# Decoder step on one core: 32 modulation steps spread over units 1 to 37 of the prompt attention, and the choice of the sample's blocks moved from units 10-16 to 18-27

## The chip, the cores and the metric

The kernel runs on one core of a Trainium2 chip. The metric is the device time of one execution in microseconds (us), as the median of several runs. TensorE is called PE here, VectorE DVE, ScalarE ACT, GpSimd POOL and SyncE SP.

## The reference

One layer of a decoder is computed for a prompt of 256 tokens and for a sample group of 8 sequences with one new token each. Both share the weights. Everything is float32. What matters for this change:

```
def _layer(x, c, pos, mixer, w_ada, b_ada, norm1_g, w_in, w_br_nsa, w_br_dil, w_out, ...):
    mod = jnp.einsum('bd,de->be', jax.nn.silu(c), w_ada) + b_ada          # w_ada: 2048 x (6*2048)
    shift1, scale1, gate1, shift2, scale2, gate2 = jnp.split(mod[:, None, :], 6, axis=-1)
    h = _rmsnorm(x, norm1_g) * (1 + scale1) + shift1
    q_nsa, kv_nsa, g_nsa, q_dil, kv_dil, g_merge = _project(h, w_in, pos)
    o_nsa, o_dil, states = mixer(q_nsa, kv_nsa, g_nsa, q_dil, kv_dil)
    ...
    x = x + gate1 * mix
    h = _rmsnorm(x, norm2_g) * (1 + scale2) + shift2
    ...
    x = x + gate2 * jnp.einsum('btf,fd->btd', f, w_down)

def _mixer_sample(...):
    o_cmp, p_cmp = _cmp_attend(q_nsa, kvc, pos)
    idx = _select_blocks(p_cmp, pos, ns)          # the 16 best of 33 blocks of 64 tokens, per sequence and kv head
    ...
    o_sel = _sel_attend(q_nsa, kvg, idx, pos)     # attention over the chosen blocks only
```

`shift1` and `scale1` are needed before the projection. The other four parts of `mod` (gate1, shift2, scale2, gate2) are needed only after the attention. `w_ada` holds 2048 x 2048 float32 for each part, 16 MB.

## The kernel before

Each engine has a program of its own in `program(...)`, written out by hand; what stands later in an engine's program runs later, and engines meet by semaphores (`mark` raises one, `wait_ge(*x.at(...))` waits for it). Before the stretch of this change lies the projection (PE lines 842 to 844), which ends at about 549 us; behind it lie the sample's attention (PE lines 960 to 1107), the merge and output products, SwiGLU and the down projection.

**The prompt attention** is a list `UNITS` of `NU` = 40 units. A unit is one head and one tile of 128 queries: units 0 to 7 are the dilated heads ("d", 4 heads by 2 tiles), units 8 to 39 the 16 NSA heads ("n", by 2 tiles). Even units see 128 keys in each branch, odd ones 256. PE's loop (line 905) is a software pipeline: in iteration u it issues

- `scores(u)`: lines 875 and 876 (n) or 880 (d). It needs DVE's maximum of unit u-1, since the bank is the same;
- one **modulation step** `ada(NA1 + u)`, line 732, for u below 32;
- `probs(u-1)`: transposes of the normalized probabilities, line 888. It needs DVE's `p` of unit u-1;
- `pv(u-2)`: products with the values, line 900.

Between `scores(u)` and `probs(u)` lies a chain of DVE (mask and maximum, L1923, L1925, L1928), ACT (exponentials, L1451) and DVE again (L1931 to L1942). DVE goes through the units in order, so it starts unit u+1 only after unit u's `p`.

**Modulation steps.** There are 6 parts of 8 steps (`ADA_STEPS` = 8). A step multiplies two k tiles of silu(c) with 2 x 128 rows of `w_ada`, one load of 2 MB. The first two parts (steps 0 to 15, `NA1` = 16) are done long before. The 32 steps of this text are the last four parts; they are counted here from 0 to 31. Their weights go through three slots: SP loads step k's weights as soon as PE has done step k-3 (`ada_load`, line 530). After the eighth step of a part, ACT copies the sum out (`ada_out`, L1260), PE turns it (`ada_turn`, L743) and DVE adds the bias (`ada_mod`, L1693). The first step of the next part waits for ACT's copy.

**The choice of the sample's blocks** (`select` on DVE, lines 1838 to 1906, and some PE and ACT instructions between units) first clears and fills the sample's queries in unit 9 (`sample_q`). Then it multiplies them with the compressed keys (PE L928, L931, in bank 7), softmaxes, sums, ranks 33 blocks against each other (DVE L1894 to L1902, on 16 x 1089 elements) and makes the mask `am`. The constants for it (`c_sample`, `before_c`, lines 560 and 561) are loaded on SP's queue behind the fourteenth modulation load.

**What hangs on it.** POOL gathers the cached pages of the sample's sequences (`selected_gathers`, line 654, 2 MB each): page 0 after `sample_q`, pages 1, 2, 3 after the modulation steps 30, 31 and 29, since they land in those slots, pages 4 and up after PE has used page w-4. SP's first window load waits for `am`, the next two for the scores of unit 39 (line 564). The sample's attention on PE starts with `turn_keys(0)` (L960) after unit 39 is done.

Of the kernel before, what the change touches and what calls it, by code (L numbers as in the profile page):

```python
# [186 lines left out]
def program(nc, i_, o_, ctx, seen):  # L187
# [188 lines left out]
    ADA_PARTS, ADA_K = 6, 2  # L376
    ADA_STEPS = KT // ADA_K
# [124 lines left out]
    NU = len(UNITS)  # L502

# [184 lines left out]
    def _(pe):  # L688
# [216 lines left out]
        for u in range(NU + 2):  # L905
            if u < NU:
                scores(u)
            if u == 0:
                pe.wait_ge(*act_.at("tm", LASTN))
            if NA1 + u < NA:  # L910
                ada(NA1 + u)
            if 1 <= u <= NU:
                probs(u - 1)
            if u >= 2:
                pv(u - 2)
            if u >= ADA_STEPS + 1 and u % ADA_STEPS == 1 and u <= NA - NA1 + 1:
                if u == 17:
                    pe.wait_ge(*dve_.at("am"))
                    pe.wait_ge(*act_.at("cpt"))
                ada_turn(ADA_FIRST + u // ADA_STEPS - 1)  # L920
            if u == 11:
                pe.wait_ge(sample_const, 16)
                pe.wait_ge(kv_loaded, 32)
                pe.wait_ge(*dve_.at("sample_q"))
                pe.wait_ge(*dve_.at("mod", ADA_FIRST))
                for b2 in range(2):
                    for c in range(4):
                        mm(bank[7][32 * c:32 * c + 32, 0:NBS], qb[:, 2 * c + b2, :], kcS[:, 2 * c + b2, 0:NBS],  # L928
                           start=(b2 == 0), stop=(b2 == 1))
                pe.wait_ge(*dve_.at("gx"))  # L930
                mm(bank[7][:, P:P + 192], const("rowsel2")[0:B, :], gx[0:B, :], start=True, stop=True).then_inc(*pe_.mark("cs"))  # L931
            if u == 13:
                pe.wait_ge(*dve_.at("cp"))
                mm(bank[7][0:H, 0:NBS], const("group"), pcmp[:, 0:NBS], start=True, stop=True).then_inc(*pe_.mark("imp"))
            if u == 14:
                pe.wait_ge(*dve_.at("cpg"))
                turn(bank[7][0:NBS, P:2 * P], pcmp[:, 0:NBS], ident).then_inc(*pe_.mark("cpt"))
            if u == 16:
                pe.wait_ge(*dve_.at("sel"))
                pe.wait_ge(*act_.at("cpt"))  # L940
                mm(bank[7][:, 2 * P:3 * P], const("spread")[0:H, :], selx[0:H].rearrange("p c j -> p (c j)"), start=True, stop=True)\
                    .then_inc(*pe_.mark("spread"))
# [293 lines left out]
    def _(act):  # L1236
# [203 lines left out]
        for u in range(NU + 2):  # L1440
            if u >= ADA_STEPS and u % ADA_STEPS == 0 and u <= NA - NA1:
                ada_out(ADA_FIRST + u // ADA_STEPS - 1)
# [18 lines left out]
            if u == 12:  # L1461
                act.wait_ge(*dve_.at("cm"))
                A(pcmp[:, 0:NBS], bank[7][:, 0:NBS], ACT.Exp, bias=stat_n[:, 1:2], scale=SC_N,
                  accum_out=dstat[:, 0:1]).then_inc(*act_.mark("ce"))
            if u == 14:
                act.wait_ge(*pe_.at("cpt"))
                cp(ptc[0:NBS, :], bank[7][0:NBS, P:2 * P]).then_inc(*act_.mark("cpt"))
# [185 lines left out]
    def _(dve):  # L1653
# [189 lines left out]
        def select(u):  # L1843
# [21 lines left out]
            if u == 10:  # L1865
# [3 lines left out]
            if u == 11:  # L1869
# [7 lines left out]
            if u == 12:  # L1877
# [4 lines left out]
            if u == 13:  # L1882
# [9 lines left out]
            if u == 14:  # L1892
# [4 lines left out]
            if u == 15:  # L1897
# [6 lines left out]
            if u == 16:  # L1904
# [3 lines left out]
        for u in range(NU):  # L1908
# [48 lines left out]
            if u >= ADA_STEPS + 2 and u % ADA_STEPS == 2 and u <= NA - NA1 + 2:  # L1957
                ada_mod(ADA_FIRST + u // ADA_STEPS - 1)
            select(u)


# [279 lines left out]
```

## Time and profile before

| | us |
|---|---|
| median of 3 runs | 2106.77 (2106.63 to 2110.05) |
| the profiled execution | 2110.02 |
| its span | 2107.7 |
| PE busy in the span | 1952.0 (93%) |
| DVE, ACT, POOL busy | 977.2, 772.9, 58.4 |
| DMA moved | 512.53 MB, mean 243 GB/s |

The span is the time from the first to the last instruction of the profile. Times below count from its start. A PE row of the timeline that says "[1.45 <-DVE ...]" tells that PE sat idle for 1.45 us before it and what ended that. "PEclk" is the clock that PE was granted: 1.00 is 2.4 GHz and 0.50 is 1.2 GHz. Matmuls of float32 are recorded twice, so a step of 8 matmuls shows as x16.

### The profile page before, as it was taken

How to read it: one execution, taken by the hardware profiler on the slowest of the kernel's cores; microseconds unless marked ns; L12 is line 12 of the kernel's file. 1: busy time of each engine (PE TensorE's matmuls, PEld its weight loads, DVE VectorE, ACT ScalarE, POOL GpSimd, SP SyncE). 2: the span in 40 equal slices, each digit the busy share in tenths (PEclk: the TensorE clock that was granted, in tenths of full speed). 3: DMA queues.
4: the chain of work that ended last, by engine and by line, in shares of the span. 5: the costliest groups of instructions: out<-in, count | busy, mean ns of one | idle time of the engine just before them, and what ended most of it. 6: DMA issues, size and time to landing. Idle time of an engine off the chain costs nothing.

```text
span 2107.7 us, 36811 instructions
## 1 busy us (share of the span) xinstructions
PE 1952.0 (93%) x15765; PEld 1786.1 (85%) x15765; DVE 977.2 (46%) x1730; ACT 772.9 (37%) x1232; POOL 58.4 (3%) x108
## 2 busy tenths in 40 slices
PE   6988999999879997999999996999999999999967
PEld 3667999999645565699999996999999999999966
DVE  3355445554346532264444756344444433645425
ACT  2345333334324432253333434333333333533322
POOL 0000000000000000000000000000000000000010
PEclk9998989999989959889999997999999999999989
DMA  9981769889899916665555653686767676578791
GB/s 372 422 288 61 214 208 313 280 275 301 338 393 372 412 43 251 229 191 186 180 182 170 219 172 141 235 271 230 267 231 267 233 244 207 196 243 270 249 315 56
DMA packets 336137, 512.53 MB, mean 243 GB/s; under 512 B 8753, under 2 KB 310105, under 8 KB 319497
## 3 DMA queue, kind: packets, MB, share of 16 engines
q1 hardware_dynamic: 316146, 368.53, 52.5%
q0 software_dynamic: 5248, 125.73, 15.1%
q10 hardware_dynamic: 14640, 16.80, 2.4%
q8 instruction: 76, 1.25, 0.2%
q14 instruction: 27, 0.22, 0.0%
HBM read 504.29 MB, written 98.91 MB: 286 GB/s over the span
## 4 chain that ended last, share of the span: by engine, by line
PE 84%; DMA 9%; DVE 4%; ACT 2%; issue 1%; SPq 0%; DVEq 0%; ACTq 0%
PE bank L1129 17%; PE bank L1130 17%; PE bank L1131 17%; PE bank L842 5%; PE bank L843 5%; PE bank L844 5%; DMA piece<-in_w_ada 4%; PE bank L732 3%; PE bank L769 2%; DMA piece<-in_w_down 2%; PE bank L900 2%; PE bank L875 1%; DMA mem<-in_cache_sel_kv,runs 1%; DMA mem<-in_const 1%; PE bank L888 1%; PE bank L960 1%
## 5 line engine op out<-in xcount | busy, mean ns | idle before, releaser
L1129 PE MATMUL bank<-piece,piece 128*128 128x264 f32 x3072 | 877.8, 286 | 50.6 <-DVE piece L2050 26.0
L1130 PE MATMUL bank<-piece,piece 128*128 128x264 f32 x3072 | 877.0, 285 | 0.0
L1131 PE MATMUL bank<-piece,piece 128*128 128x264 f32 x3072 | 876.6, 285 | 0.0
L2055 DVE TENSOR_TENSOR piece<-piece,piece 128x2048 fp32r<-128x2048 f32 (+2 forms) x216 | 440.9, 2054 | 504.5 <-ACT piece L1541 504.5
L1129 PEld LDWEIGHTS bank<-piece,piece 128*128 128x128 f32 x3072 | 582.4, 190 | 52.2 <-DVE piece L2055 24.6
L1541 ACT CAST piece<-piece 128x2048 fp32r<-128x2048 f32 (+2 forms) x216 | 368.7, 1715 | 589.0 <-PE bank L1131 509.6
L1131 PEld LDWEIGHTS bank<-piece,piece 128*128 128x128 f32 x3072 | 582.4, 190 | 0.0
L1130 PEld LDWEIGHTS bank<-piece,piece 128*128 128x128 f32 x3072 | 582.0, 189 | 0.0
L842 PE MATMUL bank<-piece,piece 128*128 128x264 f32 (+1 forms) x816 | 241.1, 295 | 0.0
L843 PE MATMUL bank<-piece,piece 128*128 128x264 f32 (+1 forms) x816 | 234.9, 288 | 0.0
L844 PE MATMUL bank<-piece,piece 128*128 128x264 f32 (+1 forms) x816 | 234.5, 287 | 0.0
L1271 ACT CAST piece<-piece 128x2048 fp32r<-128x2048 f32 (+1 forms) x51 | 96.3, 1887 | 213.2 <-PE bank L844 213.2
L842 PEld LDWEIGHTS bank<-piece,piece 128*128 128x128 f32 (+1 forms) x816 | 155.2, 190 | 1.7
L843 PEld LDWEIGHTS bank<-piece,piece 128*128 128x128 f32 (+1 forms) x816 | 155.2, 190 | 0.8
L844 PEld LDWEIGHTS bank<-piece,piece 128*128 128x128 f32 (+1 forms) x816 | 154.9, 190 | 0.2
L1713 DVE TENSOR_TENSOR piece<-piece,piece 128x2048 fp32r<-128x2048 f32 (+1 forms) x51 | 115.6, 2267 | 82.3 <-ACT piece L1271 82.2
L732 PE MATMUL bank<-piece,mem 128*32 128x512 f32 x768 | 101.8, 651 | 19.3 <-DMA piece<-in_w_ada 14.0
L1737 DVE COPY mem<-bank 64x256 f32<-64x256 f32 x128 | 54.0, 422 | 66.0 <-PE bank L758 52.4
L769 PE MATMUL bank<-mem 128*128 128x128 f32 x512 | 63.5, 285 | 7.0 <-DVE mem L1737 3.1
L732 PEld LDWEIGHTS bank<-piece,mem 128*32 128x32 f32 x768 | 21.1, 114 | 57.4 <-issue 33.5
L769 PEld LDWEIGHTS bank<-mem 128*128 128x128 f32 x512 | 61.6, 200 | 8.5 <-ACT mem L1282 5.9
L1282 ACT COPY mem<-bank 64x256 f32<-64x256 f32 x128 | 47.0, 367 | 53.0 <-PE bank L758 50.4
(324 smaller groups left out, 1449.7 us busy)
## 6 DMA issues: line engine op xcount, KB each, us to landing
piece<-in_w_ada SPq DMA_DIRECT2D x48, 2048.0 KB, 12.3
out_s_dil<-in_cache_dil_kv POOLq DMA_DIRECT2D x64, 1023.5 KB, 6.3
piece<-in_w_in SPq DMA_DIRECT2D x50, 1024.0 KB, 8.2
piece<-in_w_gate SPq DMA_DIRECT2D x22, 2048.0 KB, 8.1
piece<-in_w_up SPq DMA_DIRECT2D x22, 2048.0 KB, 8.1
piece<-in_w_down SPq DMA_DIRECT2D x32, 1408.0 KB, 6.7
piece<-in_w_in SPq DMA_DIRECT2D x16, 2048.0 KB, 8.2
piece<-in_w_out SPq DMA_DIRECT2D x8, 2048.0 KB, 8.7
```

The costliest lines, as they stand in the source:

```text
L732: last = mm(ada_banks(part_)[0][32 * j:32 * j + 32, :], siluP[:, step * ADA_K + k, :], slot(ada_slot(a), ADA_K, D)[:, k, j * 512:(j + 1) * ...
L769: last = mm(bank[0][:, sh * P:(sh + 1) * P], w1p[:, kv, l, :, :].rearrange("p j e -> p (j e)"), KS0[:, sh * 1024 + l * P:sh * 1024 + (l + ...
L842: mm(out, w_high[:, k, :], half_tile(n1_high[k]), start=(k == 0), stop=False)
L843: mm(out, w_high[:, k, :], half_tile(n1_low[k]), start=False, stop=False)
L844: last = mm(out, w_low[:, k, :], half_tile(n1_high[k]), start=False, stop=(k == KT - 1))
L1129: mm(out, w_high[:, k, :], half_tile(x_high[k]), start=(start and k == first_tile), stop=False)
L1130: mm(out, w_high[:, k, :], half_tile(x_low[k]), start=False, stop=False)
L1131: last = mm(out, w_low[:, k, :], half_tile(x_high[k]), start=False, stop=(stop and k == len(x_high) - 1))
L1271: cp(chunk_piece(chunk_high(n), n, F32R), chunk_piece(chunk_low(n), n, F32)).then_inc(*act_.mark("w_high", n))
L1541: cp(half_chunk(buffer, k_tiles), raw).then_inc(done, 1)
L1713: v.tensor_tensor(chunk_piece(a, n, F32R), chunk_piece(a, n, F32), chunk_piece(chunk_high(n), n, F32R).bitcast(F32), ALU.subtract).then_in ...
L2055: v.tensor_tensor(half_chunk(a, k_tiles, f, CW), raw, half_chunk(buffer, k_tiles).bitcast(F32), ALU.subtract)\
```

## The change

`STEP_AT` maps a unit to the step that it carries. With `NF` = 32 and `NU` - 2 = 38, step i goes to unit 1 + 38i//32: units 1 to 6, 8 to 12, 14 to 18, 20 to 25, 27 to 31 and 33 to 37. Units 0, 7, 13, 19, 26, 32, 38 and 39 carry none. `PART_END` names the units with the last step of a part: 9, 18, 28 and 37 (before: 7, 15, 23, 31). ACT's copy comes one iteration later, PE's turn two and DVE's bias three, as before; the last bias comes after DVE's loop. The choice of the sample's blocks keeps its order, but stands in units 18 (`gx`) and 22 to 27 in place of 10 to 16. `sample_q` stays in unit 9. Loads, their order on SP's queue, gathers and all sizes are the same.

```diff
+    NF = NA - NA1
+    STEP_AT = {1 + i * (NU - 2) // NF: NA1 + i for i in range(NF)}
+    PART_END = {1 + (ADA_STEPS * (i + 1) - 1) * (NU - 2) // NF: ADA_FIRST + i for i in range(NF // ADA_STEPS)}
...
# PE
-            if NA1 + u < NA:
-                ada(NA1 + u)
+            if u in STEP_AT:
+                ada(STEP_AT[u])
...
-            if u >= ADA_STEPS + 1 and u % ADA_STEPS == 1 and u <= NA - NA1 + 1:
-                if u == 17:
+            if u - 2 in PART_END:
+                if PART_END[u - 2] == ADA_FIRST + 2:
                     pe.wait_ge(*dve_.at("am"))
                     pe.wait_ge(*act_.at("cpt"))
-                ada_turn(ADA_FIRST + u // ADA_STEPS - 1)
-            if u == 11:
+                ada_turn(PART_END[u - 2])
+            if u == 22:
                 pe.wait_ge(sample_const, 16)
                 pe.wait_ge(kv_loaded, 32)
                 pe.wait_ge(*dve_.at("sample_q"))
-                pe.wait_ge(*dve_.at("mod", ADA_FIRST))
+                pe.wait_ge(*dve_.at("mod", ADA_FIRST + 1))
...
-            if u == 13:
+            if u == 24:
...
-            if u == 14:
+            if u == 25:
...
-            if u == 16:
+            if u == 27:
...
# ACT
-            if u >= ADA_STEPS and u % ADA_STEPS == 0 and u <= NA - NA1:
-                ada_out(ADA_FIRST + u // ADA_STEPS - 1)
+            if u - 1 in PART_END:
+                ada_out(PART_END[u - 1])
...
-            if u == 12:
+            if u == 23:
...
-            if u == 14:
+            if u == 25:
...
# DVE, select(u): 10 -> 18, 11 -> 22, 12 -> 23, 13 -> 24, 14 -> 25, 15 -> 26, 16 -> 27
...
-            if u >= ADA_STEPS + 2 and u % ADA_STEPS == 2 and u <= NA - NA1 + 2:
-                ada_mod(ADA_FIRST + u // ADA_STEPS - 1)
+            if u - 3 in PART_END:
+                ada_mod(PART_END[u - 3])
             select(u)
+        ada_mod(ADA_PARTS - 1)
```

How the instructions stand on PE, at three places. In the rows 32x512 x8 is one modulation step; 128x15 ends the scores of a unit, 64x128 are the products with the values. Lines of the changed kernel are three higher than those of the kernel before (735 for 732, 878 for 875, 891 for 888, 903 for 900).

First place, PE in units 11 and 12 before, where the sample's products with the compressed keys (928, 931) stand behind step 11:

```order
L732 MATMUL bank<-piece_61,mem 32x512 x8
L888 MATMUL bank<-mem 128x128 x2
L888 MATMUL bank<-mem 15x128
L900 MATMUL bank<-mem 64x128 x5
L928 MATMUL bank<-mem 32x127 x8
L931 MATMUL bank<-mem 128x192
L875 MATMUL bank<-mem 128x128 x2
L876 MATMUL bank<-mem 128x15
L732 MATMUL bank<-piece_57,mem 32x512 x8
```

The same products in the changed kernel, in unit 22 behind step 18:

```order
L735 MATMUL bank<-piece_57,mem 32x512 x8
L891 MATMUL bank<-mem 128x128 x4
L891 MATMUL bank<-mem 15x128
L903 MATMUL bank<-mem 64x128 x3
L931 MATMUL bank<-mem 32x127 x8
L934 MATMUL bank<-mem 128x192
L878 MATMUL bank<-mem 128x256 x2
```

They moved back by eleven units and seven steps.

Second place, PE around unit 26 of the changed kernel, between the steps of units 25 and 27:

```order
L735 MATMUL bank<-piece_57,mem 32x512 x8
L891 MATMUL bank<-mem 128x128 x2
L891 MATMUL bank<-mem 15x128
L903 MATMUL bank<-mem 64x128 x5
L940 MATMUL bank<-mem 127x128
L878 MATMUL bank<-mem 128x128 x2
L879 MATMUL bank<-mem 128x15
L891 MATMUL bank<-mem 128x128 x4
L891 MATMUL bank<-mem 15x128
L903 MATMUL bank<-mem 64x128 x3
L878 MATMUL bank<-mem 128x256 x2
L735 MATMUL bank<-piece_59,mem 32x512 x8
```

Two rounds of transposes and value products stand between two steps; in the kernel before there is one round between any two steps.

Third place, PE behind the last step, before:

```order
L732 MATMUL bank<-piece_59,mem 32x512 x8
L888 MATMUL bank<-mem 128x128 x2
L888 MATMUL bank<-mem 15x128
L900 MATMUL bank<-mem 64x128 x5
L875 MATMUL bank<-mem 128x128 x2
L876 MATMUL bank<-mem 128x15
L888 MATMUL bank<-mem 128x128 x4
L888 MATMUL bank<-mem 15x128
L900 MATMUL bank<-mem 64x128 x3
```

and in the changed kernel, down to the scores of unit 39:

```order
L735 MATMUL bank<-piece_59,mem 32x512 x8
L891 MATMUL bank<-mem 128x128 x2
L891 MATMUL bank<-mem 15x128
L903 MATMUL bank<-mem 64x128 x5
L878 MATMUL bank<-mem 128x128 x2
L879 MATMUL bank<-mem 128x15
L891 MATMUL bank<-mem 128x128 x4
L891 MATMUL bank<-mem 15x128
L903 MATMUL bank<-mem 64x128 x3
L878 MATMUL bank<-mem 128x256 x2
```

Before, the scores of units 32 to 39 stand behind the last step; after, those of units 38 and 39 alone.

## Rows read from the trace of the kernel before

**Rows 1.** The page's slices: granted clock and DMA share, 40 slices of 52.7 us.
```profile
PEclk9998989999989959889999997999999999999989
DMA  9981769889899916665555653686767676578791
```

**Rows 2.** Windows: stretch, length, busy PE, PEld, DVE, ACT, POOL, clock, DMA share, GB/s.
```profile
578.80:725.80 147.00, 128.38 (x928) 71.11 (x928) 75.60 (x444) 55.37 (x226) 1.97 (x2) 0.93 0.97 392
727.70:754.80 27.10, 26.18 (x117) 19.31 (x113) 13.10 (x88) 11.65 (x49) 1.88 (x2) 0.62 0.47 188
754.80:775.90 21.10, 18.84 (x71) 13.24 (x70) 7.37 (x48) 7.54 (x31) 0.00 (x0) 0.50 0.15 50
740.00:760.00 20.00, 20.00 (x75) 14.82 (x74) 9.85 (x67) 8.44 (x36) 0.00 (x0) 0.50 0.03 10
660.00:720.00 60.00, 59.32 (x447) 32.91 (x443) 30.58 (x209) 27.99 (x118) 0.00 (x0) 1.00 1.01 410
```

**Rows 3.** PE's timeline, steps 4 to 6 in the dilated units: start, length, operation, idle before.
```profile
573.82 1.92 PE L732 MATMUL bank<-piece,mem 128*32 128x512 f32 x16 [0.41 <-DMA piece<-in_w_ada]
578.78 1.92 PE L732 MATMUL bank<-piece,mem 128*32 128x512 f32 x16 [0.27 <-DMA piece<-in_w_ada]
583.75 1.92 PE L732 MATMUL bank<-piece,mem 128*32 128x512 f32 x16 [0.56 <-DMA piece<-in_w_ada]
```

**Rows 4.** PE's timeline, unit 11 and the step behind it.
```profile
623.99 1.08 PE L928 MATMUL bank<-mem 128*32 128x127 f32 x16 [11.67 <-DMA mem<-in_const]
...
627.31 3.64 PE L732 MATMUL bank<-piece,mem 128*32 128x512 f32 x16
```

**Rows 5.** PE's timeline, three steps in a row at the full clock (units 19 to 21).
```profile
668.32 1.93 PE L732 MATMUL bank<-piece,mem 128*32 128x512 f32 x16
670.17 0.55 PE L888 MATMUL bank<-mem 128*128 128x128 f32 x3
...
677.47 1.92 PE L732 MATMUL bank<-piece,mem 128*32 128x512 f32 x16
```

**Rows 6.** PE's timeline, units 15 and 16, where DVE ranks the blocks.
```profile
649.20 0.71 PE L875 MATMUL bank<-mem 64*128 64x128 f32 x4 [1.45 <-DVE mem L1925]
...
651.86 3.15 PE L732 MATMUL bank<-piece,mem 128*32 128x512 f32 x16 [1.83 <-ACT mem L1260]
```

**Rows 7.** PE's timeline from the last step to the sample's first transposes.
```profile
725.80 1.92 PE L732 MATMUL bank<-piece,mem 128*32 128x512 f32 x16 [1.12 <-DMA piece<-in_w_ada]
...
734.11 0.73 PE L888 MATMUL bank<-mem 128*128 128x128 f32 x3 [0.92 <-DVE mem L1942]
734.77 2.58 PE L900 MATMUL bank<-mem 128*64 128x128 f32 x10
...
744.87 0.90 PE L888 MATMUL bank<-mem 128*128 128x128 f32 x3
...
754.76 0.90 PE L888 MATMUL bank<-mem 128*128 128x128 f32 x3
```

**Rows 8.** DVE's timeline: two of the rankings, then unit 32's first and last operations.
```profile
644.34 1.27 DVE L1894 TENSOR_TENSOR mem<-mem 16x1089 f32<-16x1089 f32 x1
...
652.37 1.27 DVE L1898 TENSOR_TENSOR mem<-mem 16x1089 f32<-16x1089 f32 x1
...
730.49 0.29 DVE L1923 CUSTOM_DVE_ANT_0 mem<-bank,mem 128x128 f32<-128x128 f32 x1 [1.27 <-PE bank L876]
...
733.43 0.62 DVE L1942 TENSOR_SCALAR mem<-mem 128x128 f32<-128x128 f32 x3
```

**Rows 9.** POOL's timeline: the gathers of pages 1, 2 and 4.
```profile
722.16 0.97 POOL L654 DMA_INDIRECT mem<-in_cache_sel_kv,runs  x1 [115.83 <-PE bank L732]
728.02 0.94 POOL L654 DMA_INDIRECT mem<-in_cache_sel_kv,runs  x1 [4.89 <-PE bank L732]
...
795.46 0.94 POOL L654 DMA_INDIRECT mem<-in_cache_sel_kv,runs  x1 [65.26 <-PE bank L1010]
```

**Rows 10.** PE's timeline, the sample's first scores, where the clock rises again.
```profile
780.65 1.77 PE L971 MATMUL bank<-mem 128*32 128x512 f32 x8
```

**Rows 11.** DMA issues by line, window 578.8 to 725.8: count, KB each, us to landing.
```profile
piece<-in_w_ada SPq DMA_DIRECT2D x24, 2048.0 KB, 11.5
```

More of the change, by code:

```diff
@@ L1864, in select @@
                 v.tensor_copy(qz[:, :, 0:64:9], dqnew).then_inc(*dve_.mark("sample_q"))
-            if u == 10:
+            if u == 18:
                 dve.wait_ge(sample_const, 16)
@@ L1868, in select @@
                                 const("pairof")[0:B].unsqueeze(2).broadcast_to([B, 4, 48]), ALU.mult).then_inc(*dve_.mark("gx"))
-            if u == 11:
+            if u == 22:
                 dve.wait_ge(*pe_.at("cs"))
@@ L1876, in select @@
                     .then_inc(*dve_.mark())
-            if u == 12:
+            if u == 23:
                 dve.wait_ge(*act_.at("ce"))
@@ L1881, in select @@
                 v.tensor_scalar(pcmp[:, 0:NBS], pcmp[:, 0:NBS], dstat[:, 0:1], None, ALU.mult).then_inc(*dve_.mark("cp"))
-            if u == 13:
+            if u == 24:
                 dve.wait_ge(*pe_.at("imp"))
@@ L1891, in select @@
                 link(v.tensor_tensor(sc, sc, const("force")[0:H], ALU.add))
-            if u == 14:
+            if u == 25:
                 dve.wait_ge(order_loaded, 16)
@@ L1896, in select @@
                 link(v.tensor_reduce(rank, rk[0:H], AX.X, ALU.add))
-            if u == 15:
+            if u == 26:
                 link(v.tensor_tensor(rk[0:H], other, mine, ALU.is_gt))
@@ L1903, in select @@
                                 const("selmask")[0:H].unsqueeze(2).broadcast_to([H, 4, 32]), ALU.mult).then_inc(*dve_.mark("sel"))
-            if u == 16:
+            if u == 27:
                 dve.wait_ge(*pe_.at("spread"))
```

## The prediction, made before the changed kernel had run

> **What bounds the kernel now.** I began with the page's slices [rows 1]: PE's granted clock is 9 or 8 tenths nearly everywhere, but 5 in the slice from 738 to 790 us, and the DMA share of that slice is 1. So I cut the prompt attention into windows [rows 2]. There are three regimes in it. First, up to the last modulation step (578.8 to 725.8 us is the part that I sum), DMA is the busiest: share 0.97, with PE busy for 128.4 of 147.0 us. Inside that, from 660 to 720 us, PE is busy for 59.3 of 60 us at clock 1.00 while DMA stands at 1.01: the two are balanced. Second, behind the last step, PE is still busy (20.00 of 20.00 us from 740 to 760) but at clock 0.50, 1.2 GHz, and DMA is at 0.03. Third, in the sample's attention the clock rises again with the first 512-column scores [rows 10]. So weights stream while the attention's small matmuls and the steps share PE, and when the stream ends, eight units are left that run alone at half the clock. The chance lies there, and in the single waits inside the first regime: 11.67 us for the constants of the block choice [rows 4], and 1.45 and 1.83 us around the ranking [rows 6].
>
> **Prices of the pieces.** A step takes 1.85 us at full clock, from its start to the next row's start (668.32 to 670.17), and two rounds of step plus unit take 9.15 us (668.32 to 677.47) [rows 5]. So a unit's own PE work is (9.15 - 2 x 1.85) / 2 = 2.72 us at the full clock. At half clock two units without steps take 754.76 - 744.87 = 9.89 us, 4.95 each [rows 7]. The weights of a step land every 4.96 us where PE waits for them (573.82, 578.78, 583.75) [rows 3]; 24 such loads are issued in the summed window [rows 11].
>
> **Part 1, the spread.** Steps 0 to 5 sit in units 1 to 6 in place of 0 to 5, and the loads set their pace as before, so I let step 5 start at 578.8 us in both. From there to step 31 the old kernel passes 26 units and the new one 31 (units 6 to 37). Five units more cost 5 x 2.72 = +13.6 us in this window; none of them has other cover, since PE is the limit there. What it takes away is everything behind the last step up to where unit 37's step now stands, 727.7 to 754.8: -27.1 us. Those are six rounds; five of them reappear in the window, and the sixth lies before step 5, where PE waits for weights in any case.
>
> **Part 2, the constants.** SP still issues them behind the fourteenth load, around 606 us, but the first user on PE moves to unit 22, seven steps and eleven units later. The wait of 11.67 us goes, and so does the low clock that follows on it: the step behind it took 3.64 us instead of 1.92 [rows 4], and the units' work beside it about as much again. I take -11.7 and -3.9 us. What is late next is the stream itself. In the window DMA moved at 392 GB/s; at the 410 that it shows from 660 to 720 us [rows 2] the same bytes need 147.0 x 392 / 410 = 140.5 us, against the 145.8 us of PE that I get below. So PE is last by some 5 us, and single steps will still wait for weights, above all where page 0's gather (2 MB, behind `sample_q` in unit 9) goes between the loads. I take 2.5 us for these, in place of the 2.5 us or so that the old kernel has (1.12 us at the last step [rows 7] among them): 0.
>
> **Part 3, the ranking moves to units 25 and 26.** DVE's five long ranking operations (1.27 us each [rows 8]) stand in two groups: three long ones, 3 x 1.3 = 3.9 us with the gaps, and two long ones with three short ones, some 3.3 us. Each group queues before the next unit's maximum, and PE's next scores and behind them everything in its queue wait for that. Before, a step in each of the two units covered part; the stalls were 1.45 + 1.83 = 3.3 us. Now unit 26 is one of those without a step, so 1.85 us of cover is gone. A unit's chain on DVE and ACT takes 3.6 us (730.49 to 734.05 [rows 8]), of which the first 1 is the maximum; I take 3.9 for odd units. Counted from the end of unit 25's scores, DVE is through its chain at 3.9, through the first group at 7.8, has unit 26's maximum at 8.8, its chain at 11.6 and the second group at 14.9. PE would want unit 26's maximum (for the scores of 27) at 1.85 + 2 x 2.7 - 0.8 = 6.5: stall 2.3. Then, with a step and most of a round, it wants the result of the second group at 13.6: stall 1.3, and the next maximum after that: 0.5. Together 4.1 us, +0.8. The low clock after the stall (a step of 3.15 us in place of 1.92 [rows 6]) stays once: 0. If all cover were lost, it would be 3.9 + 3.3 = 7.2 us, +3.9.
>
> **Part 4, units without a step among the others** (7, 13, 19, 26, 32). Does the DVE and ACT chain stall PE there? Between a unit's scores and its transposes PE has one round and one step, 2.72 + 1.85 = 4.6 us (for unit 13 the step is that of unit 14), more than the 3.6 to 3.9 us of the chain. So 0, beyond unit 26.
>
> **Part 5, the tail.** Behind the last step stand units 38 and 39 and the drain. Before, the same work took 754.8 to 775.9 = 21.1 us at clock 0.50 [rows 2]. After its last step the old kernel kept the full clock for about 7 us more (727.7 to 734.8: rows of 2.58 us for ten matmuls begin at 734.77 [rows 7]). So the first two rounds take 5.5 us in place of 9.9, a chain wait of about 1 us shows up (0.92 before [rows 7]), and the rest stays at half clock, some 11 us with the last turn: 17.5 us, -3.6. With no fall of the clock it would be about 15.
>
> **The sum.** Window: 147.0 + 13.6 - 11.7 - 3.9 + 0.8 = 145.8 us. Old, from step 5 to the sample's first transposes: 147.0 + 48.2 (727.7 to 775.9) = 195.2. New: 145.8 + 17.5 = 163.3. The gain is 31.9 us, rounded to 32. Behind it nothing keeps an absolute time. Pages 1 to 3 are now gathered 19 to 24 us before the sample's attention instead of 48 to 54 (722.16 and 728.02 [rows 9]); three pages at about 5 us each are there in time, and the gather of page 4 follows PE's use of page 0, as before [rows 9]. So the span goes from 2107.7 to 2075.7 us. The profiled execution (2110.02) lies 3.25 us above the median (2106.77); I take the gain off the median: **2075 us**.
>
> **Two rules of the Trainium skill against this.** (1) The rows show 410 GB/s over 60 us [rows 2]. The Trainium skill, "DMA: Bandwidth & Descriptors", section "Where 436 GB/s comes from", says that for transfers from HBM to SBUF the HBM side binds at about 358 GB/s. By that rule the stream and not PE would end last, and most of the gain would be gone (rival B); the trace does not agree. (2) PE is busy for all of 740 to 760 us at clock 0.50 [rows 2]. The Trainium skill, "TensorE: Matmul & The Clock Gate", section "What's actually happening", lists idleness as what brings back the lower level. By it the tail and the units without a step would stay at 2.4 GHz, and the sum would be 2 to 3 us lower; the trace does not agree, since PE worked there.
>
> **Rivals.**
> A: the clock falls at the units without a step too. For it: it fell behind the last step with PE nearly busy. Against it: it held for 7 us there, and two rounds between steps are 5.5 us. Price: 3 us for each of the four that I left out, 12 us: 2087; with a longer stall at the ranking 2090.
> B: the stream ends last. If loads ran 13% below 410 GB/s, the window would be 140.5 x 1.15 = 161 us and the gain 17 us: 2090.
> C: the clock stays at 1.00 through the tail: 15 in place of 17.5, and the sample's first scores run at it too: 2071.
> D, the other side: with steps spread thinner the clock falls in the NSA units and stays down, as it did for the eight units at the end. Two rounds would take 9.9 + 2 x 3.64 = 17.2 us in place of 9.15, 4 us more each; 25 of them are 100 us, less the 32: 2175. It decides from 8 such rounds on. Against it: steps brought the clock back after 627 and 652 us.
> E: nothing is gained since a later stage holds an absolute time. Nothing of the kind shows in the rows; 2107.
>
> **Chances.** Forecast (2072 to 2081) 0.60, C 0.13, A 0.16, B 0.04, D 0.04, E 0.03. A measurement of this kernel can tell some 0.2% (4 us). Faster by more: 0.93; within: 0.03; slower: 0.04. The range takes in C with 3 us to spare, the forecast and A and B: 2068 to 2090.
>
> **What the new profile would show.** The wait of 11.67 us before PE's products with the compressed keys is gone. Step 31 starts near 724 us, little off 725.8, and the sample's first transposes near 744 (775.9 before). The stretch at clock 0.50 behind the last step shrinks from some 48 us to about 16. Waits of 4 us in all stand around unit 26. The gathers of pages 1 and 2 are issued near 720 and 725. I am wrong if the clock shows 0.50 near units 13, 19 or 32, if steps wait for weights by more than 5 us in all behind unit 7, or if the sample's attention waits for pages 1 to 3.

## The result

| | before | after |
|---|---|---|
| median, us | 2108.41 (4 runs, 2106.63 to 2110.45) | 2075.55 (4 runs, 2072.84 to 2080.57) |
| profiled execution, us | 2110.02 | 2076.5 |
| its span, us | 2107.7 | 2074.7 |
| mean granted clock | 0.950 | 0.964 |

The ratio after to before is 0.9847, with a 95% interval of 0.983 to 0.9865: 1.5% faster. The forecast was 2075 us. The three rows of the page that answer to [rows 1] and to the table of before:

```profile
PE 1929.0 (93%) x15765; PEld 1774.5 (86%) x15765; DVE 976.7 (47%) x1730; ACT 772.7 (37%) x1232; POOL 58.4 (3%) x108
...
PEclk9998989999999989799999989999999999999989
DMA  9981769899899855755656545676777766677791
```

The slices are 51.9 us long here. The low one of before, with clock 5 and DMA share 1, is gone: the fifteenth slice, 726 to 778 us here, has clock 8 and DMA share 5. The windows that answer to [rows 2] (stretch, length, busy PE, PEld, DVE, ACT, POOL, clock, DMA share, GB/s):

```profile
576.80:725.20 148.40, 139.24 (x1018) 80.14 (x1021) 85.69 (x522) 65.96 (x276) 1.97 (x2) 0.98 0.95 387
727.00:743.30 16.30, 12.46 (x79) 8.81 (x75) 6.74 (x42) 7.38 (x31) 1.88 (x2) 0.87 0.96 397
```

The window from step 5 to step 31 takes 148.4 us, nearly as long as before, but PE is busy for 139.2 us of it instead of 128.4. Between the end of the last step and the sample's first transposes lie 16.3 us instead of 48.2. PE's timeline of the changed kernel at its marks (start, length, operation, idle before):

```profile
548.24 0.83 PE L883 MATMUL bank<-mem 128*128 128x128 f32 x6
...
576.77 1.92 PE L735 MATMUL bank<-piece,mem 128*32 128x512 f32 x16 [0.56 <-DMA piece<-in_w_ada]
...
671.39 0.77 PE L891 MATMUL bank<-mem 128*128 128x128 f32 x5 [0.57 <-DVE mem L1945]
...
675.84 2.07 PE L878 MATMUL bank<-mem 64*128 64x256 f32 x4 [2.75 <-DVE mem L1928]
...
678.08 3.43 PE L735 MATMUL bank<-piece,mem 128*32 128x512 f32 x16
...
725.15 1.92 PE L735 MATMUL bank<-piece,mem 128*32 128x512 f32 x16
...
743.30 4.82 PE L963 MATMUL bank<-mem 128*128 128x128 f32 x20 [0.35 <-ACT mem L1439]
```

**The measure for what follows.** The first row is unit 0's scores, the last one the sample's first transposes. The stretch between them is 743.30 - 548.24 = 195.06 us. In the kernel before its start is

```profile
550.09 0.83 PE L880 MATMUL bank<-mem 128*128 128x128 f32 x6
```

and its end 775.91, so 225.82 us: the stretch became 30.8 us shorter. The other 1.9 us up to the difference of the ends (32.6) lie ahead of the stretch, in code that is the same in both. They are scatter from one execution to the next: the start of the stretch lies between 546.4 and 555.4 us in the profiles below, and the medians of one kernel differ by some us between chips. The stretch itself repeats: a second profile of the changed kernel gave 747.53 - 552.45 = 195.08 us. Edits of a few us are therefore judged by the stretch, and the times stand beside it. Behind the stretch lie 1331.8 us before and 1331.4 after: nothing was given back there.

The stretch has one weakness. It ends where the sample's first transposes start, and how long they then take hangs on the clock: 4.7 us in the changed kernel (743.30 to the next row at 748.04), 3.4 in a run below that had the full clock there (750.71 to 754.09). So a later mark is read beside it, the last transposes of the sample's scores (L988 before, L991 after). The last number behind "to" is where they start:

```profile
L988 PE MATMUL bank<-mem x16: 272/273/476, 791.1 to 851.1; 128*128 128x128 f32 x16
```
```profile
L991 PE MATMUL bank<-mem x16: 272/273/476, 758.5 to 817.8; 128*128 128x128 f32 x16
```

From unit 0's scores to there the kernel before takes 851.1 - 550.1 = 301.0 us and the changed one 817.8 - 548.2 = 269.6 (269.5 in its second profile). A table at the end of the experiments has both measures for every run.

### The profile page after: what moved, and what is told of

Its sections match the earlier page's. It is cut to its first block, busy times and chain, and to the rows that moved or that the text cites. A ratio compares the mean times of both kernels' runs of the same rounds, so it can differ in the third digit from the quotient of the medians.

```text
span 2074.7 us, 36811 instructions
## 1 busy us (share of the span) xinstructions
PE 1929.0 (93%) x15765; PEld 1774.5 (86%) x15765; DVE 976.7 (47%) x1730; ACT 772.7 (37%) x1232; POOL 58.4 (3%) x108
## 4 chain that ended last, share of the span: by engine, by line
PE 84%; DMA 9%; DVE 4%; ACT 3%; issue 1%; SPq 0%; DVEq 0%; ACTq 0%
PE bank L1132 18%; PE bank L1134 18%; PE bank L1133 18%; PE bank L845 5%; PE bank L846 5%; PE bank L847 5%; DMA piece<-in_w_ada 5%; PE bank L735 3%; PE bank L772 2%; DMA piece<-in_w_down 2%; PE bank L903 1%; DMA mem<-in_cache_sel_kv,runs 1%; PE bank L963 1%; PE bank L878 1%; PE bank L800 1%; DMA mem<-in_x_sample 1%
## 5 line engine op out<-in xcount | busy, mean ns | idle before, releaser
L735 PE MATMUL bank<-piece,mem 128*32 128x512 f32 x768 | 97.3, 626 | 17.3 <-DMA piece<-in_w_ada 14.0
```

What stands on the lines that cost most here:

```text
L735: last = mm(ada_banks(part_)[0][32 * j:32 * j + 32, :], siluP[:, step * ADA_K + k, :], slot(ada_slot(a), ADA_K, D)[:, k, j * 512:(j + 1) * ...
```

## The experiments

Each edit is against the kernel named; line numbers shift by a few.

### Each half alone

The spread alone, with the block choice as early as it can stand:

```diff
-            if u == 22:      # PE, products with the compressed keys
+            if u == 13:
...                            # gx 18 -> 12, then 23..27 -> 14..18
-                if PART_END[u - 2] == ADA_FIRST + 2:
+                if PART_END[u - 2] == ADA_FIRST + 1:
```

> One part alone: the steps spread over units 1 to 37 as in the change, the block choice as early as it can stand with them (its products with the compressed keys in unit 13, ranking in units 16 and 17, mask in 18). Theory M (PE's own work, its waits and the clock set the end of the prompt attention): PE reaches unit 13 near 610 us and waits for the constants until about 624, some 12 us; the waits for weights behind it (4.7 us in the changed kernel) go in exchange; time 2084 to 2091, the sample's first transposes near 755. Rival S (the stream of weights sets the end, PE's waits are hidden behind it): 2076 to 2079, first transposes near 745.

Measured: 2093.11 us against 2110.67 on that chip, ratio 0.9907 (0.9889 to 0.9925). The stretch is 758.93 - 551.24 = 207.69 us: 18.1 less than before, 12.6 more than in the changed kernel. PE's timeline:

```profile
625.17 1.07 PE L931 MATMUL bank<-mem 128*32 128x127 f32 x16 [10.76 <-DMA mem<-in_const]
...
628.50 3.64 PE L735 MATMUL bank<-piece,mem 128*32 128x512 f32 x16
```

The wait for the constants is there again, with the slow step behind it. It is not hidden by the stream, as rival S had it. The waits for weights in the stretch are 5.4 us in place of the changed kernel's 8.6, a part of what was to go in exchange. The time is 2 us above the expected range; with the chip's base 2 us higher as well, it is at its upper end.

The block choice alone, with the steps in units 0 to 31:

```diff
-            if u == 11:      # PE, products with the compressed keys
+            if u == 19:
...                            # gx 10 -> 18, then 12..16 -> 20..24
-                if u == 17:
+                if u == 25:
```

> The other part alone: steps in units 0 to 31 as before, the block choice moved back to units 18 to 24 (products with the compressed keys in unit 19). Theory M: the wait of 11.7 us and the low clock behind it go, but steps in every unit are then held by the weights, one per 4.96 us, so step 31 starts near 715 instead of 725.8, and the stretch at half clock behind it is 48 us as before: time near 2097, first transposes near 765. Rival (all of the gain is the spread): 2108.

Measured: 2102.06 us against 2110.67, ratio 0.996 (0.994 to 0.998). The stretch is 769.28 - 554.87 = 214.4 us, 11.4 less than before; 214.9 had been expected (765 - 550.1). PE's waits for weights on the way, in its timeline:

```profile
583.47 1.92 PE L732 MATMUL bank<-piece,mem 128*32 128x512 f32 x16 [0.28 <-DMA piece<-in_w_ada]
588.43 1.92 PE L732 MATMUL bank<-piece,mem 128*32 128x512 f32 x16 [0.56 <-DMA piece<-in_w_ada]
...
623.23 3.51 PE L732 MATMUL bank<-piece,mem 128*32 128x512 f32 x16 [5.32 <-DMA piece<-in_w_ada]
```

Rounds with 4.6 us of work are held to the weights' 4.96: PE's waits for weights in the stretch are 14.3 us in place of 8.4. So without the spread the removed wait and its low clock buy less than their 16 us, since the stream is the next limit. Up to step 31 the run is 7.7 us shorter (722.83 - 554.87 = 167.96 against 725.80 - 550.09 = 175.71). The other 3.7 of the 11.4 us are in the tail, where the clock stayed up for some 17 us behind the last step, 7 in the kernel before. Its first 15 us:

```profile
724.70:740.00 15.30, 13.04 (x91) 9.83 (x87) 9.60 (x65) 8.40 (x37) 1.87 (x2) 1.00 0.85 352
```

A shorter tail had not been expected, and it bears on the tail's forecast below. The two halves give 18.1 + 11.4 = 29.5 us alone and 30.8 together; by the later mark 19.2 + 14.1 = 33.3 alone and 31.4 together. They add, to within 2 us either way.

### Is it the clock?

```diff
+            if 34 <= u < NU:          # kernel before; in the changed one: if u >= 38
+                for n in range(8):
+                    mm(bank[6][32 * (n % 4):32 * (n % 4) + 32, :], siluP[:, n, :],
+                       xT.rearrange("p j t -> p (j t)")[:, n * 512:(n + 1) * 512], start=True, stop=True)
```

> The kernel before with eight more matmuls of 512 columns (the shape of one step, results unused, inputs already in place) in each of the units 34 to 39: 6 x 1.85 = 11 us of added PE work at full clock. Theory M (the last units are dear for the clock alone): the clock comes back within a few us, a unit takes 2.72 + 1.85 = 4.6 us instead of 4.95, and the drain and the sample's first keys run at full clock: 2102 to 2106, no slower than before in spite of the added work. Rival (the last units are slow for their own chain on DVE and ACT or their weight loads, whatever the clock): 11 to 22 us are added, 2119 to 2130.

Measured: 2100.45 us against 2110.67, ratio 0.9962 (0.9939 to 0.9985). With six times eight matmuls added, the kernel before is not slower. The stretch is 773.35 - 548.61 = 224.74 us, 1.1 less than without them. The same 26 us before (first row) and with the added matmuls (second row), as windows:

```profile
744.00:770.00 26.00, 24.96 (x93) 18.40 (x92) 12.08 (x80) 10.51 (x45) 0.00 (x0) 0.50 0.12 42
```
```profile
744.00:770.00 26.00, 24.78 (x182) 13.69 (x182) 12.06 (x80) 11.75 (x49) 0.00 (x0) 1.00 0.12 42
```

PE does 182 instead of 93 matmuls in the same time, at clock 1.00 instead of 0.50, with much the same DVE and ACT work. So the last units were dear for the clock, and a busy PE did not bring it back. The Trainium skill ("TensorE: Matmul & The Clock Gate", section "What's actually happening") lists idleness as what brings the lower level; the first of the two rows does not agree. The expected time was 2102 to 2106. Of the 10.2 us by which this run is below the kernel before, only 1.1 are in the stretch; 7.2 more come between it and the later mark, where the same instructions ran at a higher clock (before first, then this run):

```profile
775.90:851.10 75.20, 61.73 (x657) 40.52 (x658) 23.19 (x53) 23.68 (x49) 3.75 (x4) 0.85 0.50 189
```
```profile
773.30:841.30 68.00, 55.52 (x656) 36.78 (x657) 23.06 (x53) 23.54 (x49) 3.75 (x4) 0.95 0.55 209
```

That the added matmuls bring this later gain too is not shown: one profile has it, and other runs vary there by some us (71 to 77).

> The changed kernel with the same eight matmuls of 512 columns in PE's iterations 38 to 41, 7.4 us of added work. Theory M: they fill the idle 3.8 us of the tail and keep the clock at 1.00 there and through the sample's first keys, which gives back some 4.5 us: 2071 to 2077. Rival (the clock of the tail is not worth anything): 2080 to 2083.

Measured: 2081.07 us, ratio to the kernel before 0.9849 (0.983 to 0.9867), no different from the changed kernel's 0.9847 in its own run. The stretch is 750.71 - 552.29 = 198.42 us, 3.3 more than the changed kernel. The sample's first transposes and scores then run at the full clock. The time itself lies in the rival's range, but the kernel before ran at 2110.67 us on this chip, 3.9 above the base of the forecasts, and the ratio says that nothing was gained or lost. The stretch alone misleads here, since what the clock gives back to the sample's first transposes lies behind it: by the later mark the run takes 269.8 us against 269.6. So, as far as one profile tells, the 7.4 us of added work are paid back by the filled waits and the clock (a worthless clock would leave 3.6 of them), but nothing is left over: in this tail the filler is no gain.

### What sets the pace inside: the gather, the ranking, the gaps

The changed kernel again, as the measure of these:

> The changed kernel once more, on the chip and in the hour of the next three, as their measure: ratio to the kernel before 0.985, first transposes of the sample near 743 us.

Measured: 2081.38 us against 2109.08, ratio 0.9882 (0.9848 to 0.9916); the runs on this chip scatter more (before: 2097 to 2122 us). The stretch is 195.08 us, as above.

```diff
                     pool.wait_ge(*dve_.at("sample_q"))          # page 0
+                    pool.wait_ge(*pe_.at("ada", NA - 5))        # second kernel: NA - 2
```

> The changed kernel with the gather of page 0 (2 MB) put behind modulation step 27 instead of behind the sample's queries in unit 9. In the changed kernel the gather goes at 595.4 us between the loads of steps 10 to 12, and PE waits 1.48, 0.24, 2.17 and 0.83 us for weights at the four steps from 604.7 to 633.7. Theory M (the gather makes these waits and PE, not the stream, is last at the end): they shrink to about 1 us together, first transposes near 740, time 3 to 4 us below the changed kernel. Rival S (the stream is last at the end of it all): the waits only move to the last steps, no gain.

Measured: 2080.07 us, ratio 0.9879 (0.9848 to 0.9909); stretch 748.15 - 550.90 = 197.25 us, 2.2 more than the changed kernel, and the same as it by the later mark (269.5). Rival S was right about this one: behind step 27 the gather stands in front of the last weights, and PE's timeline shows

```profile
722.53 3.64 PE L736 MATMUL bank<-piece,mem 128*32 128x512 f32 x16 [3.57 <-DMA piece<-in_w_ada]
```

> The changed kernel with the gather of page 0 behind modulation step 30, where page 1's stands, so that no page goes between the weights of the steps. Theory M (PE's waits for weights in the first half, 4.7 us, come from that gather, and the stream has time to spare at the end): they shrink to 1 us and none appears later, stretch 191 to 192; the page lands before the sample's first transposes, or costs up to 3 us there. Rival S (the earlier run with this gather behind step 27 had 3.6 us of waits for weights at the last steps since the stream is as late as PE): the stretch stays at 195.

Measured: 2077.64 us against 2109.04, ratio 0.9852 (0.9828 to 0.9876); stretch 738.64 - 548.01 = 190.63 us, 4.4 less and a little under what was expected (191 to 192); 4.6 less by the later mark. PE's waits from the stretch's start to its end, the changed kernel first, then this one:

```profile
PE bank L735 <- DMA piece<-in_w_ada: 8.6, 8, 2.2
```
```profile
PE bank L736 <- DMA piece<-in_w_ada: 3.9, 4, 1.8
```

and from 590 to 660 us, where the gather had been (the changed kernel first):

```profile
590.00:660.00 70.00, 64.75 (x488) 37.28 (x485) 38.05 (x251) 31.36 (x134) 1.00 (x1) 1.00 1.01 420
```
```profile
590.00:660.00 70.00, 69.47 (x526) 39.99 (x523) 41.12 (x271) 33.94 (x147) 0.00 (x0) 1.00 1.01 420
```

DMA moves 420 GB/s in both. What differs is what it carries: with the page out of the way, PE has 4.7 us more to do in that window, and no wait comes back at the end. So PE was last at the end of the changed kernel, but by less than the 5 us that I had put down: a page behind step 27, which holds up the stream by about one step's load of 4.96 us, made PE wait for 3.57. By that the stream had some 1.4 us to spare (an estimate from these two numbers).

```diff
             if u == 25:                       # DVE: two long operations, then one, one, one with the short ones
                 ... is_equal; times before
-                reduce
-            if u == 26:
+            if u == 26:
+                reduce
+            if u == 27:
                 is_gt
+            if u == 28:
                 reduce; add; is_lt; selx
```

> The changed kernel with DVE's ranking in four pieces, in units 25 to 28 (two long operations, one, one, one with the short ones) instead of two pieces in 25 and 26; the mask in unit 29. Theory M (the ranking's DVE work is what stalls PE at unit 26, 0.57 + 2.75 us, and the stall is what drops the clock from 674.6 to 681.5 us, some 2.5 us more): the stall shrinks to about 1 us, the clock stays, first transposes near 739, time 4 to 5 us below the changed kernel. Rival 1 (the clock falls at the unit without a step whatever the ranking does): a fall near 675 stays, 2 to 3 us are gained. Rival 2 (stream of weights last): nothing.

Measured: 2079.11 us, ratio 0.9879 (0.9849 to 0.991); stretch 743.53 - 549.29 = 194.24 us, only 0.8 less. The wait of 2.75 us went down to 1.43, yet the clock fell at the same place, and a second time at 607 us behind a wait of 2.25 us for weights. By this run alone rival 1 could be right, that the unit without a step brings the clock down. The next two test that.

```diff
-    (step of unit 27)
+    STEP_AT[26] = STEP_AT.pop(27)
```

> The changed kernel with one step moved, from unit 27 to unit 26, so that both units with the ranking's stall have a step and unit 27 has none. Measured from unit 0's first scores to the sample's first transposes, the changed kernel takes 195.05 and 195.08 us in two profiles. Theory M (a step of 1.85 us covers as much of the ranking's stall, and the clock falls when PE waits and has no 512-column step): the stall of 0.57 + 2.75 us goes down to some 1.5 to 2, the clock's fall of 6.8 us vanishes or is half as long; stretch 191.5 to 193.5. Rival (the stall depends on DVE alone): 195.

Measured: 2080.11 us, ratio 0.9861 (0.983 to 0.9891); stretch 744.24 - 546.40 = 197.84 us, 2.8 more, of which 1.2 in the tail. A miss. The stall only moved: 1.53 us before the scores of 27, then 1.70 us before the transposes of unit 26, since unit 27 now had no step to cover them. The clock was low for some 10 us there, and longer in the tail too, where it fell 7 us behind the last step:

```profile
733.92 2.58 PE L904 MATMUL bank<-mem 128*64 128x128 f32 x10
```

```diff
-            if u == 25: / if u == 26:         # DVE, the two pieces of the ranking
+            if u == 27: / if u == 28:
-            if u == 27:                       # mask, on PE and DVE
+            if u == 29:
```

> The changed kernel with the two pieces of the ranking in units 27 and 28, which both have a step, in place of 25 and 26 (mask in 29). Unit 26 still has no step, and no ranking near it. Theory M (a unit without a step does not by itself bring the clock down): no clock of 0.50 near 675 us; a stall of 1.5 to 3.5 us near units 28 and 29; stretch 191 to 193. Rival (the unit without a step does it): a fall of the clock stays near unit 26, stretch 194 to 195.

Measured: 2075.58 us against 2109.04, ratio 0.9848 (0.9821 to 0.9875); stretch 740.72 - 546.46 = 194.26 us, 0.8 less; 191 to 193 had been expected. Windows around unit 26 (first row; its scores start at 668.3) and around the ranking (third row):

```profile
668.00:676.00 8.00, 7.42 (x53) 4.68 (x53) 4.90 (x36) 4.43 (x19) 0.00 (x0) 1.00 0.95 377
676.00:682.00 6.00, 4.85 (x36) 2.59 (x36) 5.64 (x16) 0.79 (x4) 0.00 (x0) 1.00 0.93 351
683.20:689.60 6.40, 4.98 (x23) 1.59 (x24) 5.31 (x21) 2.07 (x7) 0.00 (x0) 0.51 0.71 268
```

Unit 26 still has no step, and the clock stays at 1.00 there. The fall went with the ranking. That rules the unit without a step out as a sufficient cause; the stretch alone would not, since it lies in the rival's range. What stays at unit 26 is a wait of 0.58 us (0.57 in the changed kernel), though the ranking is gone from there: DVE's preparation of it in unit 24 (L1887 to L1894) was not moved and stands just ahead. So of the 3.3 us around unit 26 in the changed kernel the ranking's own share is the 2.75. The gain stayed small since the stall took its clock along: two waits of 1.15 and 1.47 us and a step of 3.64 us.

> The two edits of the last two runs together: ranking in units 27 and 28, page 0's gather behind step 30. If the two gains are of different places, they add: stretch 187 to 190, time 5 to 8 us below the changed kernel. If PE gets ahead of the stream by the first, the weights take some of it back: 191 to 193.

Measured: 2076.55 us against 2109.04, ratio 0.9837 (0.9812 to 0.9863); stretch 744.30 - 555.39 = 188.91 us, 6.2 less than the changed kernel. The two edits add to what one would have from each (4.4 + 0.8), and 1 us more, since the low clock beside the ranking was shorter. It has the lowest ratio of all that ran, but its interval overlaps the changed kernel's; that it is faster is shown for the stretch, not for the whole. By the later mark 3.6 us are left (266.0 us), and the run with page 0 moved alone stands at 265.0: the page's move shows by both measures, the ranking's by the stretch alone.

> The changed kernel with the same 32 steps as 16 pairs, in units 1, 3, 5, 8, 10, 12, 15 and so on to 36: stretches of two and three rounds without a step between pairs. PE's work is the same. If the clock falls after some 7 us without 512-column matmuls (as at 734.7 us in the kernel before), it falls in several of the stretches of three rounds (8.2 us) and in few of two (5.4 us): +2 us each, five of them, and the DVE and ACT chain stalls PE by about 1 us in each three-round stretch; first transposes 753 to 760. If what brings it down is PE's idleness alone, the clock stays at 1.00 where no wait is seen, and the transposes come at 746 to 750.

```diff
+    PAIRS = NF // 2
+    STEP_AT = {1 + j * (NU - 2) // PAIRS: NA1 + 2 * j for j in range(PAIRS)}
...
                 ada(STEP_AT[u])
+                ada(STEP_AT[u] + 1)
```

Measured: 2100.82 us, ratio 0.9954 (0.9928 to 0.998); stretch 766.84 - 552.96 = 213.88 us, 18.8 more than with single steps, for the same work. PE waited for DVE's probabilities seven times, 8.9 us in all (changed kernel: 3.0), and for weights 10.8 us (8.6), 4.71 of them at one pair. Three windows of this kernel at low clock:

```profile
618.00:624.00 6.00, 5.52 (x24) 2.13 (x25) 0.00 (x0) 0.00 (x0) 0.00 (x0) 0.50 1.00 418
632.00:638.00 6.00, 6.00 (x25) 2.87 (x28) 2.79 (x20) 2.53 (x11) 0.00 (x0) 0.50 0.19 75
690.00:699.00 9.00, 7.55 (x32) 3.92 (x34) 7.46 (x21) 1.94 (x9) 0.00 (x0) 0.50 0.28 118
```

and between them at the full one:

```profile
640.00:689.00 49.00, 46.62 (x356) 27.89 (x352) 25.99 (x174) 22.63 (x97) 0.00 (x0) 1.00 0.96 396
700.00:750.00 50.00, 46.92 (x349) 27.44 (x341) 26.08 (x180) 23.87 (x101) 2.84 (x3) 1.00 0.91 360
```

These three falls each come with a wait of PE (4.71, 1.76 and 1.93 us), and so do two more, at 571 us (4.23) and at 750 us (1.66), from where the clock stayed low to the end of the stretch. The two windows at 1.00 hold several stretches of two and three rounds without a step, with waits of 0.92 and 0.93 us, and kept the clock. So length alone did not bring it down, against the first expectation. The second was right that the clock stays where no wait is seen, but its 746 to 750 us were far off, since it left out how many long waits the pairs would make. The run cost more than the upper end of what was expected: an even spread matters for the chain of DVE and ACT as well as for the clock.

**Both measures for every run.** From unit 0's scores to the sample's first transposes (the stretch), and to the last transposes of its scores (the later mark), in us:

| | stretch | to the later mark |
|---|---|---|
| before | 225.8 | 301.0 |
| changed kernel, two profiles | 195.1, 195.1 | 269.6, 269.5 |
| spread alone | 207.7 | 281.8 |
| block choice alone | 214.4 | 286.9 |
| before, with added matmuls | 224.7 | 292.8 |
| changed, with added matmuls | 198.4 | 269.8 |
| page 0 behind step 27 | 197.3 | 269.5 |
| page 0 behind step 30 | 190.6 | 265.0 |
| ranking in four pieces | 194.2 | 268.9 |
| step moved from unit 27 to 26 | 197.8 | 272.7 |
| ranking in units 27 and 28 | 194.3 | 269.2 |
| ranking moved, page 0 behind step 30 | 188.9 | 266.0 |
| 16 pairs | 213.9 | 290.0 |

Between the two marks every run has the same instructions, yet takes 68 to 77 us there. What holds by both columns is safe from the clock at one mark.

## Why the prediction was right, point by point

**The window from step 5 to step 31** was put at 145.8 us and took 148.4 (576.77 to 725.15); step 31 was put near 724 and started at 725.15. Its terms:

- Five units more at 2.72 us, +13.6: right. The new kernel's pairs of rounds between steps in a row take the same 9.15 us (711.33 to 720.48), and PE's busy time in the window rose by 10.9 us although 3.9 us of slow clock went and 0.9 came: 10.9 + 3.9 - 0.9 = 13.9.
- The constants' wait and the slow clock behind it, -11.7 - 3.9: right. No wait stands before the products with the compressed keys, and the run with the early choice brought 10.76 us of it back, 12.6 us of stretch in all.
- Waits for weights, put at 2.5 us: they were 4.7 (1.48 + 0.24 + 2.17 + 0.83). This is the term most mis-sized, by 2.2 us; the sum lies just under the 5 us behind unit 7 that I had put down as a sign of being wrong. I had named its cause, page 0's gather between the loads, but not its price; the run with that gather moved behind step 30 removed 4.7 us of waits.
- The ranking's stall, put at 4.1 us (2.3 + 1.3 + 0.5): 0.57 + 2.75 = 3.3, of which 0.57 is not the ranking's, as the run with it moved shows. Nor was all of the 3.3 us of before: the 1.83 us are a step's wait for ACT's copy at the end of a part, which costs 0.56 and 0.53 us at the other two part ends. But the low clock beside it lasted longer than before (0.52 over the window 674.7 to 681.4): a step of 3.43 us and scores of 2.07, some 2.5 us in place of 1.6.

So +2.2 for the weights, -0.8 and +0.9 at the ranking: 2.3 of the 2.6 us by which the window came out longer. Step 5 in turn began 2.0 us earlier than in the kernel before, the stretch's start having been earlier by 1.9.

**The tail** was put at 17.5 us and took 16.3. The sum was near, but the reason was not sound, and that it came so near was luck. I had let the clock fall 7 us behind the last step, as before. It fell some 12 us behind it, near 739.5 (1.00 in the window 734 to 739, 0.50 from 739.6 to 743.3), after waits of 0.88 and 1.56 us. In the run of the spread alone it did not fall at all over the same work:

```profile
742.00:758.90 16.90, 13.09 (x91) 8.40 (x90) 7.78 (x49) 8.17 (x33) 1.87 (x2) 1.00 0.97 406
```

Both have the same instructions and the same waits there (0.17, 0.88, 1.57 and 0.88 us, against 0.17, 0.88, 1.56 and 0.88). In the run with one step moved to unit 26 it fell 7 us behind the last step of the same tail, and behind the last step of the block choice alone it held for some 17 us of small matmuls. So when the clock falls in such a tail is not settled by the work alone, and what settles it stays open. From the start of step 31 to the sample's first transposes the runs with this tail took 16.9 to 19.4 us, so a forecast should carry some 2.5 us for it.

**Units without a step** (rival A) did not bring the clock down: units 7, 13, 19 and 32 kept it. Two of them as windows:

```profile
578.60:584.00 5.40, 5.40 (x47) 4.94 (x47) 1.89 (x8) 1.95 (x5) 0.00 (x0) 1.00 1.02 423
...
702.00:707.00 5.00, 5.00 (x37) 3.90 (x40) 3.13 (x23) 2.83 (x14) 0.00 (x0) 1.00 0.97 362
```

Only unit 26 saw a fall, with the ranking's wait in it. No wait for DVE or for ACT's exponentials appears at the others, as worked out in part 4.

**The stream** (rival B): 387 GB/s over the window and 420 where it is pushed; it stays where [rows 2] had it. The 358 GB/s of the Trainium skill ("DMA: Bandwidth & Descriptors", section "Where 436 GB/s comes from") does not bind here. **Rival D** (clock down for good) and **rival E** (nothing gained) did not come: the ends moved by 32.6 us and the whole by 32.9. **The gathers** of pages 1 and 2 were issued at 722.71 and 727.38 (put at 720 and 725). The sample's attention waited for none of the pages 1 to 3. It waited for pages 4 and 6, whose gathers follow PE's use of pages 0 and 2, for 2.86 + 5.12 = 8.0 us; in the kernel before it was 3.50 + 4.06 = 7.6:

```profile
772.00 1.09 PE L963 MATMUL bank<-mem 128*128 128x128 f32 x8 [2.86 <-DMA mem<-in_cache_sel_kv,runs]
...
792.30 4.76 PE L963 MATMUL bank<-mem 128*128 128x128 f32 x20 [5.12 <-DMA mem<-in_cache_sel_kv,runs]
```
```profile
805.28 4.29 PE L960 MATMUL bank<-mem 128*128 128x128 f32 x20 [3.50 <-DMA mem<-in_cache_sel_kv,runs]
...
824.30 4.76 PE L960 MATMUL bank<-mem 128*128 128x128 f32 x20 [4.06 <-DMA mem<-in_cache_sel_kv,runs]
```

**How near the number came** is in part luck. The window was 2.6 us longer than its sum and the tail 1.2 shorter, so the stretch gained 30.8 us where 31.9 had been worked out. The medians differ by 32.9, since the profiles' starts and the medians themselves scatter by 2 us and more.

Where the gain of 30.8 us in the stretch is from, then: the experiments put 18.1 us on the spread with the constants' wait left in and 11.4 on the moved block choice alone, 3.7 of them from a clock that fell later in the tail. The 1.3 us left over are within what the two measures differ by.

## What to carry to other kernels

Small matmuls that run alone at half clock cost nearly twice their price (4.95 us a unit in place of 2.72), though PE shows as busy. Wide ones that wait for a stream anyway are best dealt out evenly among them, so that few of the small ones are left over when the stream ends. A wait on such a path should be moved only after looking at what is next: here it was the stream of weights, and a 2 MB gather between its loads cost some 4.5 us wherever it stood. Measure edits of a few us between two marks of the trace when whole runs scatter by 4 us, and look at a second mark further on before you believe 2 us.

## What the runs showed that I had not expected

- In a nearly full PE row the clock can stay at 0.50 (24.96 of 26.00 us busy), and 11 us of added 512-column matmuls cost nothing there: 182 recorded matmuls took the time of 93.
- Waits of 1.4 us and more beside steps with nothing wide in between went with falls of the clock that lasted up to 10 us; the same step-free work without the wait did not (unit 26 in the run with the ranking moved). There are exceptions: the changed kernel kept 1.00 through a wait of 2.17 us for weights (628.33) that ended in a step, and its tail fell while that of the spread alone did not, with waits of 0.9 and 1.6 us in both. So this is a leaning, not a rule.
- Against the run with it behind the loads, one page of 2 MB cost 4.4 us of stretch between the early loads and 6.6 us between the late ones (195.06 and 197.25 against 190.63), but 4.6 and 4.5 by the later mark. So the 2 us between the two places do not hold by the second measure.
- The 75 us behind the stretch, the same instructions in every run, took 68.0 us at clock 0.95 in one run and 75.2 at 0.85 in another.
